# Two-layer hybrid decoder trunk on one core: weight low parts, modulation sums and a buffer placed elsewhere

## What is computed

```python
mod = c_act @ w_mod[l] + b_mod[l]; sh1, sc1, gt1, sh2, sc2, gt2 = split(mod, 6)
h = rmsnorm(x, norm1_g[l]) * (1 + sc1) + sh1
z = h @ w_cat                                   # 3 gates, branches A, B and C
ya = rglru_branch(...)                          # conv, gated scan, GeLU
yb = diff_attention(...)                        # 4 heads, two softmax maps each
yc = rwkv7_mix(...)                             # 8 heads, a state carried in time
#  layer 1: v = v + (v_first - v) * sigmoid(v0 + shifted(z_vd) @ v2)    the value gate
#  kk = k * k_k, divided by its norm over each head
merged = sigmoid(z[0:D]) * (ya @ w_merge_a) + sigmoid(z[D:2D]) * (yb @ w_merge_b) + sigmoid(z[2D:3D]) * (yc @ w_merge_c)
x = x + gt1 * (merged @ w_out[l])
x = x + gt2 * gated_mlp(rmsnorm(x, norm2_g[l]) * (1 + sc2) + sh2)
```

## Time and profile before

| | us |
|---|---|
| median of 3 runs | 1181.33 |
| lowest and highest | 1172.01, 1183.9 |
| the profiled execution | 1186.7 |
| its span in the profile | 1184.9 |
| mean granted TensorE clock in it | 0.971 |
| PE busy | 1148.3 |

### The profile page before, as it was taken

One profiled execution on the slowest core, in us unless ns is written; L12 is line 12 of the kernel. 1 busy time (PEld: TensorE's weight loads), 2 busy tenths in 40 slices (PEclk: granted clock), 3 DMA queues, 4 the chain that ended last, 5 costly groups with the idle time before them and its releaser, 6 DMA issues.

```text
span 1184.9 us, 24153 instructions
## 1 busy us (share of the span) xinstructions
PE 1148.3 (97%) x10114; PEld 1039.0 (88%) x10114; DVE 825.1 (70%) x1223; ACT 574.9 (49%) x885; POOL 134.2 (11%) x142
## 2 busy tenths in 40 slices
PE   8989999999999999999999999999999999999997
PEld 7879987888769999999988889878876899999996
DVE  4698989465267789887635789866633867788763
ACT  2255567622064666663432475673223656666533
POOL 0010000056003000001110000002530120000001
PEclk9998999999699999999999999999997999999999
DMA  9965545244044566668835555352511455444650
GB/s 380 323 217 190 178 145 238 81 146 143 1 165 160 210 213 230 217 237 293 299 132 188 178 178 208 127 198 74 197 56 71 163 214 193 177 177 177 217 210 36
DMA packets 40953, 214.35 MB, mean 181 GB/s; under 512 B 7681, under 2 KB 8065, under 8 KB 21537
## 3 DMA queue, kind: packets, MB, share of 16 engines
q1 hardware_dynamic: 29344, 171.13, 39.9%
q0 software_dynamic: 11520, 41.95, 10.3%
HBM read 212.01 MB, written 1.05 MB: 180 GB/s over the span
## 4 chain that ended last, share of the span: by engine, by line
PE 90%; DVE 6%; issue 2%; ACT 1%; DMA 1%; DVEq 0%; ACTq 0%; SPq 0%
PE ps L1669 15%; PE ps L1670 15%; PE ps L1671 15%; PE ps L1682 7%; PE ps L1858 5%; PE ps L1860 5%; PE ps L1864 5%; PE ps L1962 5%; PE ps L1638 2%; PE ps L1654 1%; DVE macc L1056 1%; DVE RLO L1266 1%; PE ps L2051 1%; PE ps L2141 1%; PE ps L2054 1%
## 5 line engine op out<-in xcount | busy, mean ns | idle before, releaser
L913 ACT ACTIVATE WH<-ring 128x1024 fp32r<-128x1024 f32 x144 | 151.6, 1058 | 179.7 <-PE ps L1671 164.7
L1538 DVE TENSOR_TENSOR WLO<-ring,WH 128x1024 fp32r<-128x1024 f32 x144 | 175.7, 1229 | 81.8 <-ACT WH L913 81.8
L1669 PE MATMUL ps<-HH,WH 128*128 128x256 f32 x736 | 208.3, 283 | 0.0
L1670 PE MATMUL ps<-HL,WH 128*128 128x256 f32 x736 | 208.3, 283 | 0.0
L1671 PE MATMUL ps<-HH,WLO 128*128 128x256 f32 x736 | 208.3, 283 | 0.0
L1669 PEld LDWEIGHTS ps<-HH,WH 128*128 128x128 f32 x736 | 141.3, 192 | 0.0
L1670 PEld LDWEIGHTS ps<-HL,WH 128*128 128x128 f32 x736 | 141.3, 192 | 0.0
L1671 PEld LDWEIGHTS ps<-HH,WLO 128*128 128x128 f32 x736 | 141.3, 192 | 0.0
L533 POOL DMA_DIRECT2D mring<-wmod_dram x80 | 43.7, 547 | 780.6 <-DVE macc L1056 452.2
L1669 PE MATMUL ps<-GH,WH 128*128 128x256 f32 x384 | 108.9, 284 | 0.0
L1670 PE MATMUL ps<-GL,WH 128*128 128x256 f32 x384 | 108.7, 283 | 0.0
(11 more groups left out here) (397 smaller groups left out, 2536.4 us busy)
## 6 DMA issues: line engine op xcount, KB each, us to landing
ring<-wmain_dram SPq DMA_DIRECT2D x150, 1024.0 KB, 4.9
mring<-wmod_dram POOLq DMA_DIRECT2D x80, 512.0 KB, 4.8
G<-wmod_dram SPq DMA_DIRECT2D x3, 1024.0 KB, 9.5
R<-wmod_dram SPq DMA_DIRECT2D x3, 1024.0 KB, 17.4
TK<-wmod_dram SPq DMA_DIRECT2D x2, 1024.0 KB, 21.0
X<-x_t_dram SPq DMA_DIRECT2D x1, 1024.0 KB, 5.3
SW<-small_dram SPq DMA_DIRECT2D x2, 512.0 KB, 9.8
y_dram<-H SPq DMA_DIRECT2D x4, 256.0 KB, 2.2
```

The lines of the kernel that those rows point to most:

```text
L913: A(WH[:, n % 2, part], ring[:, b, part], ACT.Copy).then_inc(hi_ready, 1)
L1538: V.tensor_tensor(WLO[:, n % 2, part], ring[:, b, part], WH[:, n % 2, part].bitcast(F32), ALU.subtract).then_inc(lo_ready, 1)
L1669: MM(out, w_high[:, at], high, start=start, stop=False, skip_group_check=True)
L1670: MM(out, w_high[:, at], low, start=False, stop=False, skip_group_check=True)
```

## The change

Six things move, and nothing that is computed changes.

1. In the state steps DVE calls `dve_chunks(27 + c, 28 + c)`, so chunks 27, 28 and 29 are made after the update of steps 0, 1 and 2; behind the group norm's first part only 30 and 31 are left.
2. In each layer the two modulation blocks that stood before the first half pairs move behind `weights(1)`; chunk 13 is now made ahead of the blocks there. Sum 6l+2 is made where 6l+3 was, and 6l+3 after the last but one merge unit, with its bias added by DVE behind `gated(4)`.
3. `keep_clock` has 3, 1 and 2 matmuls in place of 5, 5, 3 and 2.
4. Sum 1 stands two matmuls later within pair 1, and the shift products stand in pair 2, ahead of its last matmul.
5. The value gate is held in `LRI`, and ACT's wait for `v_ready` goes.
6. Out pair 1's low part is made by DVE, not POOL, and out pairs' low parts are made in halves of K: first halves of pairs 0 and 1, then merged low parts, then second halves.

```diff
@@ POOL @@
-                pool.wait_ge(oh_ready, 4 * l + 2)
-                b = (PAIRS * l + OU + 1) % 4
-                pool.tensor_tensor(RLO[:, b, :], ring[:, b, :], OWH[1].bitcast(F32), ALU.subtract).then_inc(ol_pool, 1)
@@ ACT @@
-                        A(E[:, j, :], duo(6 + j // 2)[:, j % 2, :], ACT.Tanh, scale=0.5,
+                        A(LRI[:, j, :], duo(6 + j // 2)[:, j % 2, :], ACT.Tanh, scale=0.5,
...
                 act.wait_ge(kk_raw, 4 * l + 4)
-                if l:
-                    act.wait_ge(v_ready, 2)
@@ DVE @@
-                mod_beside(2)
 
                 def half_pairs_low(a, b):
...
                 half_pairs_low(2, 4)
-                mod_vector(6 * l + 2)
...
                 dve_chunks(12, 13)
                 weights(1)
+                dve_chunks(13, 14)
                 mod_beside(2)
-                dve_chunks(13, 16)
+                dve_chunks(14, 16)
+                mod_beside(2)
...
                 dve_chunks(16, 17)
-                mod_vector(6 * l + 3)
+                mod_vector(6 * l + 2)
...
-                        dve_chunks(26 + c, 27 + c)
+                        dve_chunks(27 + c, 28 + c)
...
-                dve_chunks(29, 32)
+                dve_chunks(30, 32)
...
                 gated(4)
-                out_low(0)
+                mod_vector(6 * l + 3)
+                out_low(0, 0)
+                out_low(1, 0)
                 merged_low(0)
                 merged_low(1)
                 gated(5)
+                out_low(0, 1)
+                out_low(1, 1)
                 merged_low(2)
                 merged_low(3)
-                out_low(2)
-                out_low(3)
+                for j in (2, 3):
+                    out_low(j, 0)
+                    out_low(j, 1)
@@ PE @@
-                        if used is not None and (m, i) == (1, 3):
+                        if used is not None and (m, i) == (1, 5):
                             mod_sum(1)
+                        if column and (m, i) == (1, 6):
+                            shift_column()
...
-                    keep_clock(5, 5, X[:, 0, :])
                     mod_direct(3)
-                    keep_clock(5, 5, X[:, 0, :])
+                    keep_clock(3, 5, X[:, 0, :])
                     mod_direct(7)
-                    keep_clock(3, 5, X[:, 0, :])
+                    keep_clock(1, 5, X[:, 0, :])
                     mod_sum(0)
...
                 product(l, 6, H)
-                pe.wait_ge(lora_act, 10 * l + 8)
-                mod_sum(6 * l + 2)
...
                     if n == 0:
-                        mod_sum(6 * l + 3)
+                        mod_sum(6 * l + 2)
...
                 pe.wait_ge(gn_rt, 2 * (l + 1))
+                mod_sum(6 * l + 3)
```

More of the change, by code:

```diff
@@ L434, in trunk_kernel @@
         kk_max = sem("kk_sum_bounded")
-        ol_pool = sem("out_weights_low_by_pool")
         bon_biased, bon_gated = sem("bonus_biased"), sem("bonus_gated")
@@ L1207, in _ @@
                     dve.wait_ge(zv_up, 7)
-                    V.tensor_scalar(E[:, :, :], E[:, :, :], 0.5, 0.5, ALU.mult, ALU.add).then_inc(step, tick(n_step))
+                    V.tensor_scalar(LRI, LRI, 0.5, 0.5, ALU.mult, ALU.add).then_inc(step, tick(n_step))
                     after()
-                    V.tensor_tensor(E[:, :, :], E[:, :, :], VF, ALU.mult).then_inc(v_ready, 1)
+                    V.tensor_tensor(LRI, LRI, VF, ALU.mult).then_inc(v_ready, 1)
                     dve.wait_ge(v_ready, 1)
-                    V.tensor_tensor(V_, V_, E[:, :, :], ALU.add).then_inc(v_ready, 1)
+                    V.tensor_tensor(V_, V_, LRI, ALU.add).then_inc(v_ready, 1)
                 half_pairs_low(4, 6)
@@ L1489, in _, with out_low, part @@
                 dve_chunks(33, 36)
-                def out_low(j):
+                def out_low(j, half):
+                    def part(ap):
+                        return ap.rearrange("p (m f) -> p m f", m=2)[:, :, W * half:W * half + W]
                     dve.wait_ge(oh_ready, 4 * l + j + 1)
                     b = (PAIRS * l + OU + j) % 4
-                    V.tensor_tensor(RLO[:, b, :], ring[:, b, :], OWH[j].bitcast(F32), ALU.subtract).then_inc(ol_ready, 1)
+                    V.tensor_tensor(part(RLO[:, b, :]), part(ring[:, b, :]), part(OWH[j].bitcast(F32)), ALU.subtract).then_inc(ol_ready, 1)
                 def merged_low(k):
@@ L1671, in passes, with shift_column, product @@
                 return MM(out, w_low[:, at], high, start=False, stop=stop, skip_group_check=True)
-            def product(l, k, rhs, tiles=None, used=None):
+            def shift_column():
+                pe.wait_ge(cw_acc, 8)
+                for q in range(4):
+                    last = MM(ps[:, 5, q:q + 1], CWA[:, q, :], sm[:, ONE1:ONE1 + 1], start=True, stop=True, skip_group_check=True)
+                last.then_inc(cw_mm, 1)
+            def product(l, k, rhs, tiles=None, used=None, column=False):
                 g = PAIRS * l + k
@@ L1732, in _ @@
                     product(0, 1, H, None, h_used)
[L1733 to L1737, removed]
+                    product(0, 2, H, h_ready, None, True)
                     product(0, 3, H)
@@ L1771, in _ @@
                     pe.wait_ge(zv_ready, 1)
-                    pe.wait_ge(mod_ready, 9)
                     for j in range(4):
@@ L1792, in _ @@
                     pe.wait_ge(zv_up, 7)
-                pe.wait_ge(mod_ready, 6 * l + 3)
+                pe.wait_ge(mod_ready, 6 * l + 2)
                 for b in range(2):
@@ L1931, in _ @@
                     if n == 0:
-                        mod_sum(6 * l + 3)
+                        mod_sum(6 * l + 2)
                     if n == 3:
-                        pe.wait_ge(mod_ready, 6 * l + 4)
+                        pe.wait_ge(mod_ready, 6 * l + 3)
                     if n == 4:
@@ L2096, in out @@
                         emptied(g, j)
[L2097 to L2100, removed]
+                    pe.wait_ge(ol_ready, 8 * l + ({(0, 0): 1, (1, 0): 2, (0, 4): 3, (1, 4): 4}[j, a] if j < 2 else 2 * j + 2))
                     for m in range(2):
```

## The result

The changed kernel takes 1143.4 us in the median of 4 runs (1142.94 to 1143.91), the kernel before 1179.73 in the same comparison (1172.01 to 1183.9). The ratio is 0.969, with an interval of 0.965 to 0.973. 1148 us was forecast, in a range of 1135 to 1167. The profile before was taken in an execution of 1186.7 us, which is longer than any of these four runs.

The account below looks back on a forecast made before the run. PE, busy 97% of the span, was taken as the bound, with idle time and low clock to recover. Terms 2.5 + 7.0 + 2.4 + 3.4 + 3.1 + 25.0 - 1.2 - 3.3 = 38.9 us off 1186.7 gave 1148 us, range 1135 to 1167.

Parts of the forecast that it names:

- attention weights and turning, layer 0: PE's wait of 1.52 us for chunk 13's low part goes; 3.1 us with layer 1, bounds 1.5 and 3.1.
- State steps: Both layers: chunk waits and low clock go, 25.0 us gained after a new YCL wait of 1.8 us each.
- Pair 7, layer 0: Two blocks no longer precede the half pairs, PE's wait becomes 1.9 us: 7.0 us gained, 5.3 if the clock falls.
- Layer 0 up to pair 6: Start of layer 0: nine idle matmuls go, sum 1 begins near 36 us; 2.5 us gained, bounds 0 and 4.1.
- Low stretches: New low-clock stretches at moved sum 6l+3 and the wait before chunk 32: -3.3 us, bounds -6.6 and 0.
- Layer 1's squares: The 2.1 us wait for ACT's squares and its low stretch go, next half pair 0.3 us late: 3.4 us gained.
- Out stage: Last merge units and out product: sum 6l+3 comes in, PE's 1.1 us wait goes; -1.2 us, bounds -3.4 and 0.
- The clock stays low: Rival, 0.15: small state-step matmuls may not hold the clock up; only waits go, 8.4 not 25.0 us: 1165 us.
- VectorE behind pair 7: Rival, 0.10: VectorE becomes the bound; PE waits some 4 us in layer 0 and 1 in layer 1: 1153 us.
- Next to nothing: Rival, 0.07: low parts inside the state steps delay DVE's updates; the 25.0 us and 7.2 more are lost: 1180 us.
- slower: Rival, 0.03: blocks behind weights(1) wait for a ring of two, delaying line 1396; at 35 us to landing, 1193 or more.

Follow-up runs that it names:

- the second profile: The changed kernel, unchanged, run and profiled once more as the reference of a later set: 1146.2 us (1143.7 to 1147.0).

## Why the prediction was right

The total gain was forecast at 38.9 us from the profiled execution and is 43.7 (1186.7 to 1142.95). Between the medians of the comparison it is 36.3. So the terms together were rather too large for the median kernel, and the starting point, an execution 7 us above that median, more than made up for it: the time came out near 1148 partly by luck. By place, from the same points in the two traces, one of each kernel:

| place | forecast | measured |
|---|---|---|
| layer 0 up to pair 6 | 2.5 | 4.2 |
| pair 7, layer 0 | 7.0 | 5.2 |
| attention weights and turning, layer 0 | 1.5 | 3.0 |
| state steps and YCL, layer 0 | 14.1 | 13.6 |
| out stage, layer 0 | -0.6 | -0.7 |
| start of layer 1 | 0 | 1.5 |
| pair 7 and squares, layer 1 | 5.8 | 5.0 |
| attention weights, layer 1 | 1.6 | 1.3 |
| state steps to out stage, layer 1 | 10.3 | 9.8 |
| new low stretches | -3.3 | within the rows above |

The measured rows add up to 42.9; the other 0.8 us is rounding and the end of the program.

**State steps.** This was the main term and it held in size and mechanism. From step 1's last product to the end of the second norm sums the forecast said 18.2 us; it is 19.1. The wait for YCL was said to be 1.8 us and is 1.5. What the forecast didn't know is that the wait, needed for the low clock in every profile here, doesn't always bring it, and that the low time differs between executions. It took one profile's low time for the kernel's. With item 1 added or taken back the medians move by 18 us, not 25.

**Pair 7, layer 0.** The wait was said to be 1.9 us and is 2.1. The low stretch behind it, which I priced at 1.7 us and left out of the value, came. It came in five of the six profiles with this wait and in none of the three without. The right value was the lower one of 5.3.

**Layer 0 up to pair 6.** Here the step failed. DVE was through with the blocks at 36.14, as the forecast had it, but sum 1 begins at 36.79, because PE was not waiting: with the idle matmuls gone its clock fell at 21 us, which the forecast left out. In the second profile DVE was through at 37.36 and sum 1 began at 39.55, later than in the kernel before. Putting the nine idle matmuls back moves sum 1 by only 0.7 us from the first profile. The 4.2 us measured are 1.7 of that start, 0.8 of better order and 1.7 for the low stretch at 41 us, which went with the wait for sum 1. In the second profile the whole place gives 1.4 us (pair 6 ends at 82.82 against 84.25), and with the idle matmuls back 3.4 (80.83). The term of 2.5 was right by luck.

**Low stretches.** I charged 3.3 us for new ones. The moved sum 6l+3 and the wait for YCL had none in either profile of the changed kernel. Instead three stretches at places that the change hardly touches, at 218.7, 604.4 and 962.8 us, were absent in the first profile after, worth 1.4 to 1.7 us each. Since the second profile of the kernel before lacks two of them, and the second one of the kernel after has stretches at 209 and 922 again, these are differences between executions rather than the change. The surplus of 4.8 us over the forecast is about that.

**Layer 1's squares.** 0.4 and 0.6 us of waiting for two half pairs where 0.3 in one was said. **Out stage.** As worked out, -0.6 a layer: a sum of 1.8 us more stands in front and POOL's 1.1 us are gone.

**The rivals.** *The clock stays low*: refuted in every profile without the wait; and with half the fill as well. What it rests on holds in part: once low, the clock did not come back in these small products. *VectorE behind pair 7*: no new wait there in layer 0. *Next to nothing* and *slower*: the update of step 2 is waited for 0.4 us, and line 1396 comes without a late block. The sum under *slower* doesn't close: at 35 us to landing, 25.5 us in each layer beyond the 9.5 would make 1148 + 51 = 1199, while 1193 is the median of 1181.33 plus 12. Nothing hangs on it.

What stays open: why one wait of 2.0 us is followed by 20 low microseconds and an equal one by none. The two passages of the run with item 2 alone show that neither the length of the wait nor the work around it decides between them. Open too is what items 4 and 5 are worth in time, since neither was added or taken back alone.

## What to carry to other kernels

Where TensorE's clock is low for a long time, look for the idle time just ahead of it, not at the work in it: here moving three instructions of VectorE, 1.2 us each, one step ahead took away 8 us of waits, about half of which came back at other places, and the median fell by 18 us. Before moving work between VectorE and GpSimd, look at which begins first in the new order, because an instruction of one can stand still for the whole length of the other's. When two things end a wait within a few tenths of a microsecond, removing the one that the profile names shows the other and gives next to nothing. And read the clock in more than one execution before a low stretch goes into a forecast.

## What the runs showed of the hardware

The low clock of TensorE differs between executions of one program in which every wait is the same to 0.3 us: 20.4 and 13.6 us, or 17.1 and 17.0, in the state steps of the kernel before, and 0 in one of two equal passages of another. In the eleven runs of the kernel before in one set, half the difference in low microseconds, 12 us, is nearly all of the spread in time.

Counted over all fourteen profiles, from 30 us to the last norm: PE had 22 waits of 1.5 to 1.65 us, and the clock fell behind none; 19 of 1.98 to 2.15 us, and it fell behind 15; 16 of 2.18 us and more, and it fell behind all. The counts hold for the places of these kernels alone, and a wait isn't the only occasion: the stretches at 218.7, 604.4 and 962.8 us in the first profile stand right behind one-column sums, with no wait of over 0.3 us at hand, and come and go.

The same small products of the state steps ran through at a clock of 1.00 in 21 passages, in one of them behind a wait of 1.98 us; in the seven in which the clock had fallen ahead of them it came back only in the last step or right behind it.

A VectorE instruction of 2.28 us that began 0.4 us behind a GpSimd one of 4.97 took 6.69 us. In the opposite order VectorE lost nothing (2.28 us), and GpSimd's took 5.63 us.
